# Samples' search bits start four gv tiles later and run in the chunks; turned rows, samples' attention and the first prompt scores are interleaved

## The chip, the cores and the metric

One core of one Trainium2 chip runs the whole program. The metric is the device time of one execution in microseconds (us), the median over the runs.

## What is computed

One layer of a hybrid decoder on 1024 prompt tokens and on 32 sample tokens (8 sequences of 4). Cut to what matters here:

```python
h = modulate(rms_norm(x, norm1_g), sh_a, sc_a)
gq, gk, gv, glog, gr, dq, dk, dv, iq, ik, iw = project_heads(h, w_in, ...)   # one projection
gla_state, go = gla_scan(...)                     # gated linear attention, here in chunks of 128 tokens
sc = indexer_scores(iq, iw, ik)                   # relu(iq.ik) weighted by iw, masked by causality
_, idx = top_k(sc, 256)                           # each query attends to its 256 best keys
attn = softmax(dq . dk[idx]) @ dv[idx]            # samples: keys and values from paged caches
mix = concat([gla_output(go, gr, gla_norm_g), attn])
x = x + g_a * (mix @ w_out)
x = x + g_m * hmoe(modulate(rms_norm(x, norm2_g), sh_m, sc_m))   # 16 experts, top 2 in a group
```

## The kernel before, in words

Everything is float32 and every engine has an order of its own, written out by hand; engines meet by semaphores only. An engine does its instructions in that order, so a wait in one of them holds all that stand behind it.

**Top 256 by search.** A cut is sought for each query, bit by bit, 15 high bits and 16 low bits. VectorE does it for the prompt's tiles (`seek_high`, `seek_low`, L2069 to L2090, counting at L1994). For the samples ScalarE does it in `samp_bit` (L1614): count signs (L1621), compare (L1622), move the cut (L1624). The first 15 of the 31 sample bits stand among the gate projections. The 16th, the first low bit, waits for `s_samp_key` at 2, which VectorE raises (L2069) when it has searched all high bits and built the keys of the low ones.

**The projections.** `project(n)` (L930 to L994) makes a tile in PSUM bank n % 2 and waits until `keep(n - 2)` on ScalarE has copied the tile made in the same bank; gv is kept at L1543. The gv jobs are tile 0, a part for the samples, tiles 1 to 7 and the samples' own tile. In `keep`'s loop (L1666) a sample bit follows each of the last seven jobs (`n >= first_gr - 7`).

**The chunks (L1098 to L1188 on TensorE, L1680 to L1704 on ScalarE, L2155 to L2200 on VectorE).** For each of 8 chunks of 128 tokens, and for the samples as a ninth: scores of linear attention (L1110), turned keys (L1118, copied at L1683), the projection gr (L969, kept through a silu at L1547), in chunks 4 to 7 also a dq tile (L992), outputs (L1145, L1146), the state's update (L1166). VectorE masks the scores (L2162), does two steps of its low search, updates the state and scales the chunk before (`mix_gla`, L2108). ScalarE squares the outputs (L1697), and does two sample bits in chunk 0 and one in each later chunk. VectorE's factors for chunk 0 are ready with the scaled gq and gk (L2095, L2097).

**After the chunks.** VectorE finds the cuts and makes masks (`make_mask`). TensorE turns the samples' cached keys (`turn_k`, L1204), scores the first four sequences (`score_set(0)`, L1211), then the last four (`score_set(1)`), adds the masks and the samples' own keys (L1241 to L1244), turns the nine tiles of linear attention (`turn_mix_g`, L1232, copied by `keep_mix_g`, L1724, in banks 2 and 3) and then turns the samples' probabilities (L1251, L1252). VectorE gives the minimum of each half (L2207), ScalarE the exponents (L1732, L1734), the copies of the turned probabilities (L1742, L1743), the scaled output (L1747) and its 16 small copies into `mix_t` (L1754), after which it raises `s_o_samp_kept`.

**Prompt attention.** 64 units of a query tile and a head. TensorE makes two at a time (`score_pair`, L1263), VectorE adds the mask and takes the minimum (`mask_and_min`, L2231), ScalarE exponentiates (L1764), VectorE scales by the sum (`normalise`, L2240), TensorE turns (`turn`, L1295) and weighs (`weigh`, L1305). The first `turn` needs four scaled units. Before, TensorE makes pair 0 ahead of the samples' products (L1278); pairs 2 to 6 and VectorE's first unit stand behind `s_o_samp_kept`.

After that come the output projection (L1352), the router and 24 steps of experts (L1416 to L1452).

Of the kernel before, what the change touches and what calls it, by code (L numbers as in the profile page):

```python
# [16 lines left out]
P = 128  # L17
D = 1024
KT = D // P
SEQ = 1024  # L20
NSEQ = 8
DT = 4
NS = NSEQ * DT
NT = SEQ // P
TILES = NT + 1
TOK = SEQ + NS
PAGES = 8
PAST = PAGES * P
LS = PAST + NS
# [6 lines left out]
HD = 64  # L36
GQ = 4
# [109 lines left out]
def hybrid_decoder_step(nc, place, a, a_out):  # L147

    jobs, first_gla, first_gr, first_dq = projections()
# [9 lines left out]
    with ExitStack() as ctx:  # L159
# [103 lines left out]
        psum = ctx.enter_context(nc.psum_tensor("psum", [P, 8, 512], F32))  # L263
# [626 lines left out]
        def _(pe):  # L890
# [316 lines left out]
            def score_set(half):  # L1207
                pe.wait_ge(s_k_seq_t, SET * (half + 1))
                for c in range(2):
                    for b in range(SET * half, SET * (half + 1)):  # L1210
                        mm = pe.matmul(psum[rows_of_seq(b), 4 + 2 * half + c, :], dq_samp[:, b, :], k_seq_t[:, b % SET, c * 512:(c + 1) * 512],  # L1211
                                       start=True, stop=False)
                mm.then_inc(s_k_seq_used, 1)
# [6 lines left out]
            score_set(0)  # L1220
            for b in range(SET + 1, NSEQ):
                turn_k(b)
            score_set(1)

            def turn_mix_g(i):

                r = rows(i)
                pe.wait_ge(s_mix_g, i + 1)
                if i >= 2:
                    pe.wait_ge(s_mix_g_t, i - 1)  # L1230
                for k in range(4):
                    t = pe.transpose(psum[:, 2 + i % 2, k * r:(k + 1) * r], gv[0:r, i, k * P:(k + 1) * P], ident[0:r, 0:r])  # L1232
                t.then_inc(s_mix_g_turned, 1)


            pe.wait_ge(s_k_seq_t, NSEQ)
            pe.wait_ge(s_masks, NT - 1)
            for half in range(2):
# [3 lines left out]
                pe.matmul(psum[:, half, 0:NS], dq_samp[:, SET * half:SET * (half + 1), :].rearrange("p b r -> p (b r)"), dk_t[:, SEQ:TOK],  # L1242
                          start=True, stop=False)
                pe.matmul(psum[:, half, 0:NS], visible, score[NT][0:NS, PAST:LS], start=False, stop=True).then_inc(s_samp_scores, 1)  # L1244
            for i in range(TILES):
                turn_mix_g(i)
            pe.wait_ge(s_mix_g_t, TILES)
            for half in range(2):
                pe.wait_ge(s_p_samp_exp, half + 1)
                for p in range(PAGES):  # L1250
                    t = pe.transpose(psum[:, 4 + 2 * half + p // 4, (p % 4) * P:(p % 4 + 1) * P], p_samp[:, half, p * P:(p + 1) * P], ident)  # L1251
                t = pe.transpose(psum[0:NS, 2 + half, 0:P], p_samp[:, half, PAST:LS], ident)  # L1252
                t.then_inc(s_p_samp_turned, 1)
            def score_pair(u):

                i, g, _, _ = unit_of(u)
# [10 lines left out]


            pe.wait_ge(s_p_samp_t, 2)
            score_pair(0)  # L1270
            for half in range(2):
                o = psum[:, 4 + 2 * half, 0:P]
                pe.matmul(o, p_samp_t[0:NS, half, PAGES, :], dkv[0:NS, NT, P:2 * P], start=True, stop=False)
                for b in range(SET * half, SET * (half + 1)):
                    wait_pages(b, 2)
                for p in range(PAGES):
                    for b in range(SET * half, SET * (half + 1)):
                        mm = pe.matmul(o[rows_of_seq(b), :], p_samp_t[:, half, p, rows_of_seq(b)], pages_of(b)[:, p, :],  # L1278
                                       start=False, stop=(p == PAGES - 1))
                mm.then_inc(s_o_samp, 1)  # L1280
            for half in range(2):
                pe.wait_ge(s_o_samp_rows, half + 1)
                pe.transpose(psum[:, 5 + 2 * half, 0:P], o_samp[:, half, :], ident).then_inc(s_v_pages_used, 1)
# [14 lines left out]
            def weigh(m):  # L1298
# [7 lines left out]
                                   start=(b == 0), stop=(b == groups[k][0][slot]))  # L1306
                mm.then_inc(s_weighed, 1)

            pe.wait_ge(s_o_samp_kept, 1)
            for u in range(2, PER_GROUP, 2):  # L1310
                score_pair(u)
            OUT_PART_AT = len(turns) - 5

            def out_products():
# [161 lines left out]
        def _(act):  # L1476
# [188 lines left out]
            keep_ada(2, ada_m1)  # L1665
            for n in range(first_gv + 1, first_gr):  # L1666
                keep(n)
                if n >= first_gr - 7:
                    samp_bit(*next(samp_next))

            squared = []
# [6 lines left out]
            for c in range(TILES):  # L1678
                r = rows(c)
                act.wait_ge(s_gla_k_turned, c + 1)  # L1680
                if c >= 2:
                    act.wait_ge(s_kv, c - 1)
                act.activation(k_rows[0:r, c % 2, :, :], psum[0:r, 4, 0:2 * P].rearrange("p (j k) -> p j k", j=2), copy).then_inc(s_gla_k_kept, 1)  # L1683
                keep(job_of["gr", c, 0])
                if ("dq", c - GQ, 0) in job_of and c - GQ >= 0:
                    keep(job_of["dq", c - GQ, 0])
                if c == NT - 1:
                    keep(job_of["gr_part", 0, 0])
                if c == NT:
                    act.wait_ge(s_inter, 1)  # L1690
                    act.activation(inter_rows.rearrange("p s v -> p (s v)"), psum[:, 3, :], copy).then_inc(s_inter_kept, 1)
                act.wait_ge(s_o, c + 1)
                act.wait_ge(s_kv, c + 1)
                if c >= 1:
                    own.wait(squared[-1])
                for h in range(H_GLA):
                    n = own.did(act.activation(squares[0:r, h * DV:(h + 1) * DV], psum[0:r, 5 + c % 2, h * DV:(h + 1) * DV], ACT.Square, accum_out=ss_g[0:r, c, h:h + 1]))  # L1697
                squared.append(n)
                act.activation(gv[0:r, c, :], psum[0:r, 5 + c % 2, :], copy).then_inc(s_o_kept, 1)
                if c >= 1:  # L1700
                    rstd_gla(c - 1)
                if c < NT:
                    for _ in range(2 if c == 0 else 1):
                        samp_bit(*next(samp_next))  # L1704
            rstd_gla(TILES - 1)
            assert next(samp_next, None) is None
# [18 lines left out]
                               scale=gla_g[:, 0:1]).then_inc(s_mix_g_t, 1)  # L1725

            act.wait_ge(s_w_small, 128)
            for half in range(2):
                for i in range(3 * half, 3 * half + 3):
                    keep_mix_g(i)  # L1730
                act.wait_ge(s_samp_min, half + 1)
                act.activation(p_samp[:, half, 0:PAST].rearrange("p (c s) -> p c s", c=2), psum[:, 4 + 2 * half:6 + 2 * half, :], ACT.Exp,  # L1732
                               scale=-1.0, bias=p_min[:, half:half + 1], accum_out=p_sum[:, 2 * half:2 * half + 1])
                act.activation(p_samp[:, half, PAST:LS], psum[:, half, 0:NS], ACT.Exp,  # L1734
                               scale=-1.0, bias=p_min[:, half:half + 1], accum_out=p_sum[:, 2 * half + 1:2 * half + 2]).then_inc(s_p_samp_exp, 1)
            for i in range(6, TILES):
                keep_mix_g(i)
            act.wait_ge(s_states_out, 64)
            act.wait_ge(s_mix_g, TILES)
            for half in range(2):  # L1740
                act.wait_ge(s_p_samp_turned, half + 1)
                act.activation(p_samp_t[:, half, 0:PAGES, :].rearrange("p (c k) r -> p c (k r)", c=2), psum[:, 4 + 2 * half:6 + 2 * half, :], copy)  # L1742
                act.activation(p_samp_t[0:NS, half, PAGES, :], psum[0:NS, 2 + half, 0:P], copy).then_inc(s_p_samp_t, 1)  # L1743
            act.wait_ge(s_p_inv, 1)
            for half in range(2):
                act.wait_ge(s_o_samp, half + 1)
                act.activation(o_samp[:, half, :], psum[:, 4 + 2 * half, 0:P], copy, scale=p_sum[:, 2 * half:2 * half + 1]).then_inc(s_o_samp_rows, 1)  # L1747
            for half in range(2):
                act.wait_ge(s_v_pages_used, half + 1)
                for n in range(2):  # L1750
                    of_head = psum[n * HD:(n + 1) * HD, 5 + 2 * half, 0:P].rearrange("p (b n g t) -> p n g b t", b=SET, n=2, g=GQ)[:, n]
                    at_tokens = slice(SEQ + half * SET * DT, SEQ + (half + 1) * SET * DT)
                    for g in range(GQ):
                        kept = act.activation(mix_t[n * HD:(n + 1) * HD, 4 + g, at_tokens].rearrange("p (b t) -> p b t", t=DT), of_head[:, g], copy)  # L1754
            kept.then_inc(s_o_samp_kept, 1)

            def exponent(u):

# [21 lines left out]
            o_after = {GROUP_BLOCKS * k + (pair[0] if slot == 0 else GROUP_BLOCKS - 1) + KEPT_AFTER: (k, slot)  # L1782
                       for k, (pair, n) in enumerate(groups) for slot in range(2)}

            for u in range(PER_GROUP):
                exponent(u)
            for m, (k, slot, b) in enumerate(turns):
                step = m % GROUP_BLOCKS
# [83 lines left out]
        def _(dve):  # L1872
# [40 lines left out]
            n = 0  # L1913
# [325 lines left out]
                own.wait(own.did(dve.reciprocal(a_inv[:, u:u + 1], a_sum[:, i, head:head + 1])))  # L2239
                dve.tensor_scalar(x, x, a_inv[:, u:u + 1], None, ALU.mult).then_inc(s_prob, 1)  # L2240

            dve.wait_ge(s_o_samp_kept, 1)
            mask_and_min(0)
            mask_and_min(1)
            for u in range(len(units)):
                if u + 2 < len(units):
                    mask_and_min(u + 2)
                normalise(u)
# [209 lines left out]
```

## Time and profile before

| | us |
|---|---|
| median of 3 runs | 1238.65 (1238.35 to 3723.86) |
| profiled execution, whole | 1239.81 |
| its span, first to last instruction | 1238.1 |
| TensorE busy | 1073.4 |
| VectorE busy | 617.0 |
| ScalarE busy | 401.3 |

The mean granted clock of TensorE is 0.926 of full speed. In the rows PE is TensorE's matmuls (transposes too), DVE is VectorE, ACT is ScalarE. A float32 product of full size shows as two records. "idle before" in brackets is the time in which the engine did nothing ahead of an instruction, with the one that ended it. Times in a timeline are us from the start of the span.

### The profile page before, as it was taken

The numbers are of one execution on the slowest core, as the hardware profiler recorded it, in microseconds if no ns is written. First come the engines' busy times: TensorE is split into PE (matmuls) and PEld (weight loads), VectorE is DVE, ScalarE is ACT, GpSimd is POOL, SyncE is SP. The second block draws the span as 40 slices with busy tenths as digits, with TensorE's granted clock in tenths as the row PEclk, the third lists the DMA queues.
The fourth block names the chain that finished last, engine by engine and source line by source line (L and its number), as shares of the span: only waits on it lengthen the run. The fifth ranks groups of instructions, "written<-read, shape, count | busy, mean of one in ns | idle before, by whom it ended". The sixth has DMA issues, their size and how long they took to land. (4 is left out here: it accounts for less than half of the span.)

```text
span 1238.1 us, 15189 instructions
## 1 busy us (share of the span) xinstructions
PE 1073.4 (87%) x4998; PEld 519.6 (42%) x4998; DVE 617.0 (50%) x1311; ACT 401.3 (32%) x880; POOL 121.8 (10%) x197
## 2 busy tenths in 40 slices
PE   4799999994998998986999999994699999999910
PEld 2595433341454544453444445553333333333300
DVE  3300589999299887933666423326112222222239
ACT  5321563640544343154777611112111111111113
POOL 0302000000000000522000000000211111111041
PEclk9799999997998997987999999996699999999965
DMA  9512516520310003346200111113897774576556
GB/s 342 192 39 57 204 35 238 206 71 0 72 30 0 1 1 85 90 137 163 58 1 1 35 38 70 62 56 124 315 366 279 301 293 182 209 268 255 187 213 241
DMA packets 70486, 170.82 MB, mean 138 GB/s; under 512 B 25511, under 2 KB 39959, under 8 KB 60041
## 3 DMA queue, kind: packets, MB, share of 16 engines
q1 hardware_dynamic: 55916, 122.77, 28.3%
q0 software_dynamic: 14496, 47.12, 10.6%
q8 instruction: 40, 0.66, 0.2%
q14 instruction: 34, 0.28, 0.1%
HBM read 237.18 MB, written 23.91 MB: 211 GB/s over the span
## 5 line engine op out<-in xcount | busy, mean ns | idle before, releaser
L969 PE MATMUL psum<-mem 128*128 128x512 f32 (+4 forms) x544 | 165.0, 462 | 24.9 <-ACT mem L1543 18.9
L1428 PE MATMUL psum<-mem 128*64 128x512 f32 x768 | 173.6, 606 | 3.7 <-DMA mem<-in_w_exp_up 2.5
L992 PE MATMUL psum<-mem 128*128 128x512 f32 x320 | 140.6, 596 | 0.0
L969 PEld LDWEIGHTS psum<-mem 128*128 128x128 f32 (+1 forms) x544 | 92.7, 192 | 90.6 <-issue 64.7
L1352 PE MATMUL psum<-mem 128*128 128x512 f32 x256 | 111.1, 593 | 0.6 <-issue 0.6
L1428 PEld LDWEIGHTS psum<-mem 128*64 128x64 f32 x768 | 54.1, 139 | 105.4 <-issue 101.3
L992 PEld LDWEIGHTS psum<-mem 128*128 128x128 f32 x320 | 60.1, 190 | 78.8 <-issue 78.0
L1452 PE MATMUL psum<-mem 128*64 128x512 f32 x384 | 87.6, 598 | 2.4 <-DVE mem L2396 2.4
L2404 DVE TENSOR_TENSOR mem<-psum,mem 128x256 f32<-128x256 f32 x24 | 10.2, 425 | 150.4 <-ACT mem L1849 150.4
L1994 DVE TENSOR_SCALAR_CACHE_REDUCE marks<-mem,top_try_low 128x384 uint16<-128x384 uint16 (+2 forms) x96 | 84.5, 942 | 0.6
L1994 DVE TENSOR_SCALAR_CACHE_REDUCE marks<-mem,top_try 128x384 bf16<-128x384 bf16 (+2 forms) x90 | 79.2, 942 | 0.5
L2394 DVE SCALAR_TENSOR_TENSOR mem<-psum,mem 128x1024 f32<-128x1024 f32 x24 | 30.8, 1284 | 90.9 <-PE psum L1452 90.9
L2231 DVE CUSTOM_DVE_ANT_0 mem<-psum,mem 128x1024 f32<-128x1024 f32 (+7 forms) x64 | 48.2, 754 | 55.3 <-PE psum L1263 40.0
L1352 PEld LDWEIGHTS psum<-mem 128*128 128x128 f32 x256 | 48.2, 190 | 58.8 <-issue 58.8
L1849 ACT ACTIVATE mem<-psum 128x256 f32<-128x256 f32 x24 | 9.2, 385 | 164.8 <-PE psum L1428 164.8
L1772 ACT ACTIVATE mem<-psum 128x512 f32<-128x512 f32 x72 | 42.8, 595 | 36.0 <-PE psum L1295 35.4
L1263 PE MATMUL psum<-mem 64*128 64x512 f32 (+3 forms) x192 | 42.6, 553 | 12.8 <-DVE a_min L2231 11.3
L1764 ACT ACTIVATE mem<-mem,a_min 128x1024 f32<-128x1024 f32 (+7 forms) x64 | 49.4, 771 | 6.4 <-DVE a_min L2231 6.3
L1295 PE MATMUL psum<-const,mem 128*128 128x128 f32 x288 | 48.0, 290 | 1.9 <-DVE mem L2240 1.9
L1922 DVE TENSOR_SCALAR mem<-mem,iw 128x512 f32<-128x512 f32 (+3 forms) x10 | 4.4, 437 | 87.8 <-ACT mem L1575 87.8
L1305 PE MATMUL psum<-mem 128*64 128x256 f32 x288 | 47.0, 405 | 0.1
L1805 ACT ACTIVATE mem<-mem 128x1024 f32<-128x1024 f32 (+1 forms) x9 | 9.5, 1056 | 111.4 <-DVE mem L2271 111.4
(385 smaller groups left out, 1420.6 us busy)
## 6 DMA issues: line engine op xcount, KB each, us to landing
mem<-in_w_exp_gate SPq DMA_DIRECT2D x48, 1024.0 KB
mem<-in_w_exp_up SPq DMA_DIRECT2D x48, 1024.0 KB
mem<-in_w_exp_down SPq DMA_DIRECT2D x48, 1024.0 KB
mem<-in_w_ada SPq DMA_DIRECT2D x24, 1024.0 KB, 10.0
y_of_slot<-mem POOLq DMA_DIRECT2D x24, 512.0 KB, 4.2
mem<-in_x_prompt SPq DMA_DIRECT2D x16, 512.0 KB, 5.0
mem<-in_w_in SPq DMA_DIRECT2D x3, 2048.0 KB, 7.7
h_rows<-mem POOLq DMA_DIRECT2D x8, 512.0 KB, 2.9
```

What stands on the lines that cost most here:

```text
L969: mm = pe.matmul(bank[0:rows(i), to:to + width], h_t[:, k, cols(i)], w[:, k, c0:c0 + width], start=(k == 0), stop=(k == KT - 1))
L992: mm = pe.matmul(bank[:, 0:n_t], w[:, k, c0:c0 + P], h_t[:, k, t0:t0 + n_t], start=(k == 0), stop=(k == KT - 1))
L1263: mm = pe.matmul(psum[:, score_bank(u + n) + s0 // 512, 0:w], dq_t[kv(n), g, cols(i)], dk_t[kv(n), s0:s0 + w], start=True, stop=True)
L1295: t = pe.transpose(psum[:, 4 + m % 2, q * P:(q + 1) * P], x[:, b * P:(b + 1) * P], ident)
L1305: mm = pe.matmul(psum[kv(n), 6 + slot, 0:2 * P], dkv[:, b, P + n * HD:P + (n + 1) * HD], prob_t[:, m % 3, 2 * n * P:2 * (n + 1) * P], star ...
L1352: mm = pe.matmul(psum[0:r, 2 * (i % 2) + c, :], mix_t[:, k, cols(i)], w_out[:, k, c * 512:(c + 1) * 512], start=(k == 0), stop=(k == KT - 1))
L1428: mm = pe.matmul(psum[half_rows(half), 2 + u, :].rearrange("p (n f) -> p n f", n=2), x_slot_t[:, u, k, half_rows(half)], gate_up_w[2 * u + ...
L1452: mm = pe.matmul(psum[half_rows(half), 6 + c, :], hid_t[:, u, m, half_rows(half)], down_w[2 * u + half][:, m, c * 512:(c + 1) * 512], star ...
L1764: act.activation(x, x, ACT.Exp, scale=-1.0, bias=a_min[:, i, head:head + 1], accum_out=a_sum[:, i, head:head + 1]).then_inc(s_exp, 1)
L1772: act.activation(prob_t[:, m % 3, :], psum[:, 4 + m % 2, :], copy).then_inc(s_turn_kept, 1)
L1994: dve.tensor_scalar(marks[0:r, j % 2, 0:width].bitcast(values[j].dtype), values[j], cuts[0:r, j:j + 1], None, ALU.is_ge, ALU.add, accum_ou ...
L2231: dve.tensor_tensor_reduce(x, banks, score[i], 1.0, 3 * BIG, ALU.add, ALU.min, a_min[:, i, head:head + 1]).then_inc(s_row_min, 1)
```

## The change

Four of the samples' search bits leave the gv tiles: there, bits now follow only the last three jobs, and chunks 1 to 4 have two bits instead of one. TensorE turns two tiles of linear attention ahead of `score_set(1)`, two after each half of the sample scores, and the last three around the turned probabilities, whose last piece now goes to bank 0 or 1. `score_pair(2)` follows the samples' products of half 0; TensorE waits for `s_o_samp_kept` only after `score_pair(6)`, VectorE only ahead of unit 8. ScalarE's exponents, copies of turned rows and of the samples' output follow the new order. No DMA issue is moved.

```diff
# TensorE
-            score_set(1)
...
+            def turn_p_samp(half):
+                pe.wait_ge(s_p_samp_exp, half + 1)
+                for p in range(PAGES):
+                    pe.transpose(psum[:, 4 + 2 * half + p // 4, (p % 4) * P:(p % 4 + 1) * P], p_samp[:, half, p * P:(p + 1) * P], ident)
+                pe.transpose(psum[0:NS, half, 0:P], p_samp[:, half, PAST:LS], ident).then_inc(s_p_samp_turned, 1)
+
+            pe.wait_ge(s_k_seq_t, NSEQ - 1)
+            turn_mix_g(0)
+            turn_mix_g(1)
+            score_set(1)
             pe.wait_ge(s_k_seq_t, NSEQ)
             pe.wait_ge(s_masks, NT - 1)
             for half in range(2):
...
-            for i in range(TILES):
-                turn_mix_g(i)
-            pe.wait_ge(s_mix_g_t, TILES)
-            for half in range(2):
-                pe.wait_ge(s_p_samp_exp, half + 1)
...
+                turn_mix_g(2 + 2 * half)
+                turn_mix_g(3 + 2 * half)
+            turn_p_samp(0)
+            turn_mix_g(6)
+            turn_p_samp(1)
+            turn_mix_g(7)
+            turn_mix_g(8)
...
             pe.wait_ge(s_p_samp_t, 2)
+            pe.wait_ge(s_mix_g_t, TILES)
             score_pair(0)
             for half in range(2):
...
                 mm.then_inc(s_o_samp, 1)
+                if half == 0:
+                    score_pair(2)
...
+            for u in range(4, PER_GROUP, 2):
+                score_pair(u)
             pe.wait_ge(s_o_samp_kept, 1)
-            for u in range(2, PER_GROUP, 2):
-                score_pair(u)
# ScalarE
             for n in range(first_gv + 1, first_gr):
                 keep(n)
-                if n >= first_gr - 7:
+                if n >= first_gr - 3:
                     samp_bit(*next(samp_next))
...
                 if c < NT:
-                    for _ in range(2 if c == 0 else 1):
+                    for _ in range(2 if c < 5 else 1):
                         samp_bit(*next(samp_next))
...
+            for i in range(4):
                 keep_mix_g(i)
             act.wait_ge(s_states_out, 64)
+            exponent_samp(0)
+            keep_mix_g(4)
+            keep_mix_g(5)
+            exponent_samp(1)
             act.wait_ge(s_mix_g, TILES)
+            keep_p_samp(0)
+            keep_mix_g(6)
+            keep_p_samp(1)
+            keep_mix_g(7)
+            keep_mix_g(8)
...
+            exponent(0)
+            exponent(1)
             act.wait_ge(s_p_inv, 1)
+            keep_o_samp(0)
+            exponent(2)
+            keep_o_samp(1)
+            exponent(3)
             for half in range(2):
                 act.wait_ge(s_v_pages_used, half + 1)
...
             kept.then_inc(s_o_samp_kept, 1)
-            for u in range(PER_GROUP):
+            for u in range(4, PER_GROUP):
                 exponent(u)
# VectorE
-            dve.wait_ge(s_o_samp_kept, 1)
             mask_and_min(0)
             mask_and_min(1)
             for u in range(len(units)):
+                if u + 2 == PER_GROUP:
+                    dve.wait_ge(s_o_samp_kept, 1)
                 if u + 2 < len(units):
                     mask_and_min(u + 2)
                 normalise(u)
```

`exponent_samp`, `keep_p_samp` and `keep_o_samp` hold the same instructions that stood in ScalarE's loops over the halves; before, its order was three copies of turned rows, exponents of half 0, three copies, exponents of half 1, three copies, then the turned probabilities, the outputs and all exponents of the first eight units.

## Rows read from the trace of the kernel before

**Rows 1.** The page, busy time: us, share of the span, instructions.
```profile
PE 1073.4 (87%) x4998; PEld 519.6 (42%) x4998; DVE 617.0 (50%) x1311; ACT 401.3 (32%) x880; POOL 121.8 (10%) x197
```

**Rows 2.** Waits, 260 to 600 us: engine, line, waited for, us, times, longest.
```profile
ACT mem L1621 <- DVEq L2069: 29.4, 1, 29.4
...
PE psum L969 <- ACT mem L1543: 18.9, 1, 18.9
...
DVE mem L2231 <- ACT mem L1754: 15.3, 1, 15.3
```

**Rows 3.** Timeline of TensorE, gv tiles: start, us, instruction, idle before.
```profile
264.03 27.73 PE L969 MATMUL psum<-mem 128*128 128x512 f32 x64
310.68 22.44 PE L969 MATMUL psum<-mem 128*128 128x512 f32 x48 [18.91 <-ACT mem L1543]
...
334.02 1.48 PE L1110 MATMUL psum<-mem 64*128 64x128 f32 x8
```

**Rows 4.** Timeline of ScalarE, the first low search bit.
```profile
308.08 1.17 ACT L1621 ACTIVATE mem<-mem,samp_shift 32x1056 bf16<-32x1056 uint16 x1 [29.41 <-DVEq L2069]
...
309.70 0.29 ACT L1624 ACTIVATE samp_shift<-samp_keep,samp_shift 32x1 f32<-32x1 f32 x1
```

**Rows 5.** Timeline of VectorE, the scaled gk.
```profile
310.55 2.35 DVE L2097 TENSOR_TENSOR mem<-mem 128x2112 f32<-128x2112 f32 x1
```

**Rows 6.** Timeline of ScalarE, chunks 2, 3 and 5: table, silu of gr.
```profile
366.37 1.28 ACT L1547 ACT_TABLE_LOAD   x1 [1.73 <-DVE mem L2108]
...
382.23 1.28 ACT L1547 ACT_TABLE_LOAD   x1 [5.10 <-DVE mem L2108]
...
420.00 0.60 ACT L1547 ACTIVATE mem<-psum 128x512 f32<-128x512 f32 x1 [1.82 <-PE psum L969]
```

**Rows 7.** Timeline of TensorE, chunk 3 and the gr tile of chunk 4.
```profile
383.19 0.46 PE L1145 MATMUL psum<-mem 128*128 128x128 f32 x2 [2.97 <-DVE mem L2162]
...
391.36 9.24 PE L969 MATMUL psum<-mem 128*128 128x512 f32 x16
```

**Rows 8.** Timeline of TensorE, from sample scores to the first turned probabilities.
```profile
536.54 1.93 PE L1211 MATMUL psum<-mem 128*32 128x512 f32 x16 [1.11 <-ACT mem L1718]
...
544.06 5.08 PE L1232 MATMUL psum<-const,mem 128*128 128x128 f32 x20
...
561.16 1.99 PE L1263 MATMUL psum<-mem 64*128 64x512 f32 x8 [1.26 <-ACT mem L1743]
...
572.32 2.86 PE L1263 MATMUL psum<-mem 64*128 64x512 f32 x8 [3.76 <-DVE a_min L2231]
...
581.56 1.12 PE L1295 MATMUL psum<-const,mem 128*128 128x128 f32 x4 [1.89 <-DVE mem L2240]
582.60 3.79 PE L1263 MATMUL psum<-mem 64*128 64x512 f32 x8
```

**Rows 9.** Timeline of ScalarE, turned rows and samples' attention.
```profile
545.27 1.48 ACT L1724 ACTIVATE mem<-psum,gla_g 128x512 f32<-128x512 f32 x2 [8.78 <-PE psum L1232]
...
549.23 1.11 ACT L1732 ACTIVATE mem<-psum,p_min 128x1024 f32<-128x1024 f32 x1
...
558.22 1.03 ACT L1742 ACTIVATE mem<-psum 128x1024 f32<-128x1024 f32 x1 [2.35 <-PE psum L1252]
...
568.07 1.58 ACT L1754 ACTIVATE mem<-psum 64x16 f32<-64x16 f32 x16
```

**Rows 10.** Timeline of VectorE, samples' minimum and first units.
```profile
541.09 1.23 DVE L2207 TENSOR_REDUCE p_min<-psum 128x1 f32<-128x1024 f32 x1 [7.63 <-PE psum L1244]
...
569.79 1.23 DVE L2231 CUSTOM_DVE_ANT_0 mem<-psum,mem 128x1024 f32<-128x1024 f32 x1 [15.26 <-ACT mem L1754]
...
576.49 0.75 DVE L2240 TENSOR_SCALAR mem<-mem 128x1024 f32<-128x1024 f32 x1
```

**Rows 11.** Busy time by stretch (TensorE's alone; all engines): last PEclk, DMA, GB/s.
```profile
544.00:549.00 5.00, 4.91 (x21) 0.50 0.46 130
...
411.30:471.00 59.70, 59.36 (x212) 30.34 (x212) 45.92 (x127) 24.03 (x58) 0.00 (x0) 1.00 0.00 0
```

More of the change, by code:

```diff
@@ L1244, in _ @@
                 pe.matmul(psum[:, half, 0:NS], visible, score[NT][0:NS, PAST:LS], start=False, stop=True).then_inc(s_samp_scores, 1)
-            for i in range(TILES):
-                turn_mix_g(i)
-            pe.wait_ge(s_mix_g_t, TILES)
-            for half in range(2):
-                pe.wait_ge(s_p_samp_exp, half + 1)
[L1250 to L1253, printed above, removed]
+                turn_mix_g(2 + 2 * half)
[5 more added lines that the diff above has]
+            turn_mix_g(8)
             def score_pair(u):
@@ L1727, in _, with exponent_samp @@
             act.wait_ge(s_w_small, 128)
-            for half in range(2):
-                for i in range(3 * half, 3 * half + 3):
-                    keep_mix_g(i)
+            def exponent_samp(half):
                 act.wait_ge(s_samp_min, half + 1)
@@ L1735, in _, with keep_p_samp @@
                                scale=-1.0, bias=p_min[:, half:half + 1], accum_out=p_sum[:, 2 * half + 1:2 * half + 2]).then_inc(s_p_samp_exp, 1)
-            for i in range(6, TILES):
+            def keep_p_samp(half):
+                act.wait_ge(s_p_samp_turned, half + 1)
+                act.activation(p_samp_t[:, half, 0:PAGES, :].rearrange("p (c k) r -> p c (k r)", c=2), psum[:, 4 + 2 * half:6 + 2 * half, :], copy)
+                act.activation(p_samp_t[0:NS, half, PAGES, :], psum[0:NS, half, 0:P], copy).then_inc(s_p_samp_t, 1)
@@ L1737, in _, with keep_o_samp @@
+            def keep_o_samp(half):
+                act.wait_ge(s_o_samp, half + 1)
+                act.activation(o_samp[:, half, :], psum[:, 4 + 2 * half, 0:P], copy, scale=p_sum[:, 2 * half:2 * half + 1]).then_inc(s_o_samp_rows, 1)
+            for i in range(4):
                 keep_mix_g(i)
             act.wait_ge(s_states_out, 64)
+            exponent_samp(0)
+            keep_mix_g(4)
+            keep_mix_g(5)
+            exponent_samp(1)
             act.wait_ge(s_mix_g, TILES)
[L1740 to L1754, printed above, removed]
@@ L1755, in _ @@
-            kept.then_inc(s_o_samp_kept, 1)
+            keep_p_samp(0)
[3 more added lines that the diff above has]
+            keep_mix_g(8)
             def exponent(u):
@@ L1783, in _ @@
                        for k, (pair, n) in enumerate(groups) for slot in range(2)}
-            for u in range(PER_GROUP):
+            exponent(0)
+            exponent(1)
+            act.wait_ge(s_p_inv, 1)
+            keep_o_samp(0)
+            exponent(2)
+            keep_o_samp(1)
+            exponent(3)
+            for half in range(2):
+                act.wait_ge(s_v_pages_used, half + 1)
+                for n in range(2):
+                    of_head = psum[n * HD:(n + 1) * HD, 5 + 2 * half, 0:P].rearrange("p (b n g t) -> p n g b t", b=SET, n=2, g=GQ)[:, n]
+                    at_tokens = slice(SEQ + half * SET * DT, SEQ + (half + 1) * SET * DT)
+                    for g in range(GQ):
+                        kept = act.activation(mix_t[n * HD:(n + 1) * HD, 4 + g, at_tokens].rearrange("p (b t) -> p b t", t=DT), of_head[:, g], copy)
+            kept.then_inc(s_o_samp_kept, 1)
+            for u in range(4, PER_GROUP):
                 exponent(u)
```

## The prediction

> **What bounds the kernel now.** I read four views, in this order. The page first: TensorE is busy for 87% of the span, so what can be won is TensorE's waits and its half-clock stretches; work taken off another engine is worth only what TensorE waited for it [rows 1]. Then the sums of waits between 260 and 600 us, the stretch that the diff touches. The reader is to see a ring there: ScalarE stood 29.4 us for VectorE's search keys, and TensorE 18.9 us for ScalarE, once each; and later VectorE stood 15.3 us for ScalarE's copies of the samples' attention [rows 2]. Then the timelines of the three engines, to see who was late at each place. Last, granted clock by stretch.
>
> The sum is made on the profiled execution: 1239.8 us, of which 1238.1 is its span; the median of the runs, 1238.65, is 1.2 below it.
>
> **Part 1: the search bits (gv tiles and chunks).** TensorE had finished gv tiles 1 to 4 at 291.8, 6.93 us a tile, and could not start tile 5 before ScalarE kept tile 3. ScalarE stood ahead of that copy in the first low search bit, waiting for the keys, until 308.08. So TensorE ran on at 310.68: 22.44 us for tiles 5 to 7, then 0.9 for the samples' tile, and chunk 0 at 334.02 [rows 3, 4]. The change starts the low bits behind tile 6 instead of tile 2. Then all copies that TensorE needs are made in time. Tiles 5 to 7 follow at 291.8 and take 3 x 6.93 = 20.8, to 312.6; with 0.9 for the last, chunk 0 is reached at 313.5, against 334.02: 20.5 us earlier. (18.9 is the wait; the rest is that the three tiles after it took 22.44 instead of 20.8, at a lower clock.)
>
> Two things could hold the new start. Chunk 0 needs VectorE's scaled keys gk, whose instruction begins at 310.55 and takes 2.35, so it ends at 312.9 [rows 5]: 0.6 us before TensorE comes, nothing late. And ScalarE meets its keys at 308.08, as now, but its first bit (1.95 us: 308.08 to 309.99 in [rows 4]) then ends at 310.0, before tile 7 is done at 312.6. VectorE's search itself is not touched: it idled between 312.9 and chunk 0, and that idle goes.
>
> What is added: one more bit of 1.95 us on ScalarE in each of chunks 1 to 4, ahead of the next chunk's copy of keys and its silu. What hides them is the wait that ScalarE has ahead of its silu: 1.73 us behind chunk 1's bit, 5.10 behind chunk 2's, 1.82 behind chunk 4's [rows 6]; behind chunk 3's it is like chunk 2's. So at most 0.2 shows on ScalarE, and TensorE, which then has a tile of nearly 7 us ahead of it, doesn't see it. Cost 0; if the cover failed everywhere, 4 x 1.95 = 7.8. TensorE's 2.97 us wait for VectorE in chunk 3 [rows 7] stays, because both engines start chunk 0 in the same relation as before (VectorE free first, TensorE's first product 1.5 us later). I bound it from +3 (gone) to -3 (twice). No DMA is moved by the diff; the dq weights and the sample states, loaded at the end of gv, have the same chunks of time before their use as now.
>
> **Part 2: turned rows and samples' attention.** Times are on the axis of before; part 1 shifts them all. Before, TensorE starts sample scores 1 at 536.54 after 1.11 us of waiting, turned rows run from 544.06, and prompt pair 0 starts at 561.16 [rows 8]. ScalarE's own work sets how early pair 0 can come, so I lay it out in the new order. The two rows turned ahead of scores 1 (8 transposes; 20 took 5.08 at half clock, so some 0.13 each at full) fill the 1.1 us wait and move nothing. VectorE's minimum of half 0 starts at 541.1 and is there 1.5 later, at 542.6 [rows 10]; it had stood idle 7.6 us, so the masks are no limit. ScalarE has copied four turned rows by 542.9 (0.74 each), loads its table, 1.28 (duration as in [rows 6]), and exponentiates half 0 in 1.36 (1.11 and the small second piece): 545.5. Two copies: 547.0. Half 1: 548.4. Turned half 0, 1.2 (1.03 and its small piece): 549.6. Row 6: 550.3. Turned half 1: 551.5. Rows 7 and 8: 552.7 [rows 9]. TensorE turns half 0 between 545.6 and 547.8 even at half clock, and half 1 by 550.7: hardly late. Pair 0 at 552.9 instead of 561.16: 8.2 us.
>
> **Part 3: the first prompt units.** VectorE's first masked row started only at 569.79, after 15.3 us of idle, because it waited for the last of the 16 small copies of the samples' output, which began at 568.07 and took 1.58 [rows 9, 10]. That wait moves to unit 8. Now it waits for pair 0's scores alone: 552.9 + 1.6 = 554.5, that is 15.3 earlier. From the first masked row to the first turned probabilities (581.56) it took 11.8. In the new order TensorE does samples' products of half 0 meanwhile, until 557.3, and so pair 2 begins 0.3 after its banks are free; the pair takes 1.99 like pair 0 instead of 2.86 [rows 8]. So 11.8 + 0.3 - 0.9 = 11.2, and turning starts at 565.7: 15.9 earlier in parts 2 and 3 together (8.2 and 7.7). What is late next is VectorE's chain of four masked units of 1.2 and four scalings of about 0.9 (0.75 and a reciprocal, [rows 10]); ScalarE's extra work between exponents ends, with the 16 copies, at about 565.2, so TensorE's wait for it, now ahead of the first turn, is hidden by 0.5. If that cover is gone, each us of it is paid.
>
> **The clock.** Between 544 and 549 the clock was 0.50 though TensorE was busy 4.91 of 5 us [rows 11], and pair 8 behind the first turn took 3.79 us where pair 0 of the same shape took 1.99: the lower of the two levels, 1.2 instead of 2.4 GHz, after waits of 3.76 and 1.89 us and another between them [rows 8]. The new order leaves waits of about 2 us there. I take 1 of the 1.8 us; at full clock throughout it is 1.8, at half clock from 553 on it is a loss of some 9 (2 for each of two pairs, 2.3 for each half's products).
> The Trainium skill (TensorE: Matmul & The Clock Gate, "What's actually happening") says that the throttled state is the default and that activity releases it. Taken alone it would give the whole 1.8, and the sum would be 1201.6. The row at 544 does not agree, since there the clock was low on a busy engine. That is why I don't count on it.
>
> **Sum.** 20.5 + 15.9 + 1 = 37.4. 1239.8 - 37.4 = 1202.4; I say 1202.
>
> **The rivals.**
> A. ScalarE's added bits do lie on the path of the chunks (7.8 us back): 1210. For it: in chunk 4 the cover is 1.82 against 1.95. Against: in the others VectorE is later. 12%.
> B. Half clock through the samples' stage (9 + 1 back): 1212. For it: [rows 11]. 13%.
> C. More than counted: chunk 3's wait goes too, and with it the slow stretch behind it, in which one gr tile took 9.24 us instead of 6.93 and the small products were slow too [rows 7] (3 + 4): 1195. 8%.
> D. Part 3 is hidden anyway: TensorE's wait for the samples' copies moves with it and holds the first turn as before, and parts 2 and 3 give nothing: 1239.8 - 20.5 = 1219. Against: 0.5 us of cover and a queue in which the exponents stand ahead of the copies. 4%.
> E. It does not do what it says: ScalarE's wait for the keys, now behind tile 6, is met by TensorE again because VectorE comes later, say at 314 or more, and most of part 1 stays away: about 1220. Against: nothing that VectorE does before 312.9 is moved. 2%.
> F. The other side: the chunks with dq fall to half clock. In 59.7 us there TensorE is busy 59.36, at 1.00 [rows 11]; at half they last 59.7 longer: 1202 + 60 = 1262, slower than before. It decides as soon as over 37.4 us of such work runs at half. For it: the slow tile of [rows 7]. Against: it was one tile, and this stage has the same work as before. 2%.
>
> My forecast has the other 59%. The range takes in A, B and C: 1195 to 1213. A measurement of this kernel can tell about 2% (24.8 us) from no change; faster than 1214 holds in my forecast and A to C, 92%; D and E lie within 2%, 6%; F is slower, 2%.
>
> **What would show it.** Right: no TensorE wait over 1 us among the gv tiles; chunk 0 at about 313.5; ScalarE's wait for the keys about 2 us; from the start of chunk 0 to the start of the dq jobs behind the chunks the same length as before; VectorE's first masked row 15 us earlier in relation to the turned keys, and pair 8 near 2 us. Wrong: waits of TensorE for ScalarE in chunks 1 to 4 (A), 0.50 in the clock between sample scores and first turn (B), a wait of many us ahead of the first turn (D). If parts 1 to 3 show as worked out and the time is still not near 1202, something behind 590 moved, which I hold for a plain shift.

## The result, and the profile after

The changed kernel takes 1203.76 us (median) beside 1239.12 for the kernel before; the ratio is 0.9708, 95% interval 0.9684 to 0.9732. Each of the two medians is over four executions, one of which (2967 and 3724 us) was far slower and is not in the ratio; the other three alone have medians of 1202.62 and 1238.65. The profiled execution took 1202.62, with a span of 1200.9. A second set of runs, e5 below, gave 1202.47 beside 1240.96, ratio 0.9686 (0.9670 to 0.9702). Forecast were 1202 and a range of 1195 to 1213.

The page of the changed kernel: the span, TensorE's row, which answers to [rows 1], and the granted clock in 40 slices.

```profile
span 1200.9 us, 15186 instructions
...
PE 1066.6 (89%) x4998; PEld 516.6 (43%) x4998; DVE 617.0 (51%) x1311; ACT 401.1 (33%) x880; POOL 122.4 (10%) x197
...
PEclk9799999999997997999999999995799999999965
```

The number of instructions on TensorE, VectorE and ScalarE is the same, and so, within 0.2 us, is what VectorE and ScalarE are busy for. TensorE is busy 6.8 us less with the same work, because more of it ran at the full clock. The other 30 us are time in which TensorE no longer waits.

TensorE's timeline of the changed kernel, in the places of [rows 3, 7 and 8] (start, us, instruction, idle before it):

```profile
263.14 48.33 PE L969 MATMUL psum<-mem 128*128 128x512 f32 x112
...
312.38 1.47 PE L1110 MATMUL psum<-mem 64*128 64x128 f32 x8
...
349.85 1.48 PE L1110 MATMUL psum<-mem 64*128 64x128 f32 x8
...
361.54 0.49 PE L1145 MATMUL psum<-mem 128*128 128x128 f32 x2 [2.97 <-DVE mem L2185]
...
368.20 2.49 PE L1110 MATMUL psum<-mem 64*128 64x128 f32 x8
...
371.10 9.21 PE L969 MATMUL psum<-mem 128*128 128x512 f32 x16
...
504.35 1.95 PE L1204 MATMUL psum<-const,mem 128*128 128x128 f32 x16
...
525.58 1.92 PE L1237 MATMUL psum<-const,mem 128*128 128x128 f32 x8
...
532.04 1.99 PE L1269 MATMUL psum<-mem 64*128 64x512 f32 x8 [1.37 <-ACT mem L1733]
...
545.01 0.63 PE L1304 MATMUL psum<-const,mem 128*128 128x128 f32 x4 [2.42 <-DVE mem L2263]
545.88 3.56 PE L1269 MATMUL psum<-mem 64*128 64x512 f32 x8 [0.25 <-DVE a_min L2254]
```

The gv tiles 1 to 7 are one block of 48.33 us (6.90 a tile) with no wait in it, where [rows 3] shows two blocks and 18.91 between them. Three more rows of the kernel before are needed to lay the two beside each other, the starts of chunks 3 and 4 and of the turned keys:

```profile
371.50 1.48 PE L1110 MATMUL psum<-mem 64*128 64x128 f32 x8
...
388.45 2.49 PE L1110 MATMUL psum<-mem 64*128 64x128 f32 x8
...
524.64 1.95 PE L1204 MATMUL psum<-const,mem 128*128 128x128 f32 x16
```

| stretch of the profiled execution | before | after | difference | forecast |
|---|---|---|---|---|
| start to chunk 0 | 334.0 | 312.4 | -21.6 | -20.5 |
| chunk 0 to the turned keys | 190.6 | 192.0 | +1.4 | 0 |
| turned keys to pair 0 | 36.5 | 27.7 | -8.8 | -8.2 |
| pair 0 to the first turn | 20.4 | 13.0 | -7.4 | -7.7 |
| first turn to the end of the span | 656.5 | 655.9 | -0.6 | -1 |
| span | 1238.1 | 1200.9 | -37.2 | -37.4 |

Of the 21.6, 0.9 stood already ahead of gv tile 1 (264.03 and 263.14) and has nothing to do with the change; 20.7 are part 1. The last stretch took 655.9 to 658.2 us in the traces of this document, 657.4 in the second execution of the changed kernel (e5), so its 0.6 is inside what executions differ by.

ScalarE of the changed kernel, in the places of [rows 4 and 9]:

```profile
307.18 1.17 ACT L1630 ACTIVATE mem<-mem,samp_shift 32x1056 bf16<-32x1056 uint16 x1 [1.94 <-DVEq L2092]
...
522.76 1.28 ACT L1739 ACT_TABLE_LOAD   x1
524.05 1.12 ACT L1739 ACTIVATE mem<-psum,p_min 128x1024 f32<-128x1024 f32 x1
...
525.42 1.26 ACT L1733 ACTIVATE mem<-psum,gla_g 128x512 f32<-128x512 f32 x2
...
543.00 1.58 ACT L1806 ACTIVATE mem<-psum 64x16 f32<-64x16 f32 x16
```

Its wait for the keys is 1.94 us instead of 29.41. The copies at 525.42 follow the exponents with no table load between, so mixing the two kinds of work costs no load: there is one, 1.28 us, as before. The Trainium skill (ScalarE: Activation LUTs, "Table sets: the hidden batching unit") says why that can be: cheap functions such as copy are in every set, and only a change of set costs a load. The rows here agree with it.

VectorE of the changed kernel, in the places of [rows 10]; the last row is the scaling that the first turn waits for:

```profile
520.88 1.23 DVE L2230 TENSOR_REDUCE p_min<-psum 128x1 f32<-128x1024 f32 x1 [7.72 <-PE psum L1252]
...
534.13 1.23 DVE L2254 CUSTOM_DVE_ANT_0 mem<-psum,mem 128x1024 f32<-128x1024 f32 x1 [5.69 <-PE psum L1269]
...
544.08 0.79 DVE L2263 TENSOR_SCALAR mem<-mem 128x1024 f32<-128x1024 f32 x1
```

Its 15.26 us wait for the samples' copies is now 5.69 us for pair 0's scores.

### The profile page after: what moved, and what is told of

The parts are those of the page before. It is cut to its first block and busy times, and to the rows that moved or that the text cites. A ratio compares the mean times of both kernels' runs of the same rounds, so it can differ in the third digit from the quotient of the medians.

```text
span 1200.9 us, 15186 instructions
## 1 busy us (share of the span) xinstructions
PE 1066.6 (89%) x4998; PEld 516.6 (43%) x4998; DVE 617.0 (51%) x1311; ACT 401.1 (33%) x880; POOL 122.4 (10%) x197
```

## The experiments

**Each half alone.** e1 is the kernel before with the search bits moved, e2 the changed kernel with them back:

```diff
# e1, on the kernel before
-                if n >= first_gr - 7:
+                if n >= first_gr - 3:
-                    for _ in range(2 if c == 0 else 1):
+                    for _ in range(2 if c < 5 else 1):
# e2, on the changed kernel: the same two lines the other way
```

> The kernel before with the search bits moved alone (part 1), the order of turned rows and first units as before. My theory: chunk 0 is reached some 20.5 us earlier, nothing is paid for the four bits in chunks 1 to 4 beyond up to 1.5 us of a longer half-clock stretch in chunk 3: 1239 - 20 = 1219, between 1217 and 1221. Rival A (the four bits lie on the path of the chunks): 1226. Rival E (the wait for the keys is only put elsewhere): above 1230.

> The changed kernel with the search bits at their old places (parts 2 and 3 alone). My theory: 8.5 us from sample scores to pair 0, 7.5 from pair 0 to the first turn, 0 to 1 behind it: 1239 - 16 = 1223, between 1221 and 1225, and the gains of this run and of the bits alone add up to the whole within 2 us. Rival D (part 3 hidden): 1231.

Measured: e1 1218.84 (0.9825, 0.9806 to 0.9844), e2 1221.82 (0.9857, 0.9835 to 0.9880), beside 1239.70. That is 20.9 and 17.9 us; their sum, 38.8, is the 38.5 of the second set of runs within 0.3, and 2.8 more than the 36.0 of the first (1238.65 less 1202.62). So the two halves add up as closely as the two sets agree. Rivals A (1226), E (above 1230) and D (1231) fall. In e1 VectorE's first masked row still waits for the samples' copies, even 17 us, the old wait with its full length:

```profile
549.25 1.22 DVE L2231 CUSTOM_DVE_ANT_0 mem<-psum,mem 128x1024 f32<-128x1024 f32 x1 [17.14 <-ACT mem L1754]
```

**Where the bits may start.** e3 and e4 start them behind gv tiles 4 and 5 instead of tile 6:

```diff
# e3: 5 and c < 3; e4: 4 and c < 4
-                if n >= first_gr - 3:
+                if n >= first_gr - 5:
-                    for _ in range(2 if c < 5 else 1):
+                    for _ in range(2 if c < 3 else 1):
```

> The changed kernel with the first low bit behind gv tile 4 instead of tile 6 (five bits among the gv tiles, two in chunks 0 to 2 only). My theory: ScalarE stands from tile 4's copy to the keys at 307.2, takes 1.95 for the bit, and copies tile 5 at about 309.1 to 309.7; TensorE wants its bank at 304.5 for tile 7. So TensorE waits 5.2 us and the time is 5 to 7 us above the changed kernel: 1208 to 1210. If the place of the bits among the gv tiles does not matter as I worked it out (the gain came from something else), it equals the changed kernel, 1203.

> The same with the first low bit behind gv tile 5 (four bits among the gv tiles, two in chunks 0 to 3). ScalarE then copies tile 6 at 309.7, and TensorE wants that bank only for the samples' tile at 311.4. My theory: no wait, the time equals the changed kernel within 1 us: 1203. A rival by which every tile that the bits come earlier costs its 7 us: 1206 to 1210.

Measured: e3 1210.80, just above the 1208 to 1210 that I expected, and e4 1205.18. The waits, between 255 and 600 us, of e3 and then of e4 (us in total, times, longest):

```profile
ACT mem L1630 <- DVEq L2092: 15.7, 1, 15.7
...
PE psum L969 <- ACT mem L1552: 5.2, 1, 5.2
```

```profile
ACT mem L1630 <- DVEq L2092: 8.8, 1, 8.8
```

ScalarE waits 15.7 us in e3 and TensorE 5.2 of them; in e4 ScalarE still waits 8.8 and TensorE none. That is the place from which the ring costs: two banks let TensorE be two tiles ahead, and a wait of ScalarE shorter than that lead is free. What I had left out is the clock behind the wait. The gv tile that follows it in e3 takes 8.68 us instead of 6.90, so the wait of 5.2 costs 7.0 in all:

```profile
311.80 8.68 PE L969 MATMUL psum<-mem 128*128 128x512 f32 x16 [5.17 <-ACT mem L1552]
```

e4's median is 2.6 and 2.7 above the two of the changed kernel (1202.62 and 1202.47), inside the spread of its own runs (1199.6 to 1207.1).

**What cover the four bits have.** e6 does each sign count of chunks 1 to 4 twice, which changes no result; e5 is the changed kernel itself beside it.

```diff
                         samp_bit(*next(samp_next))
+                        if 1 <= c < 5:
+                            own.wait(own.did(act.activation(samp_marks, samp_keys[1], ACT.Sign, ..., accum_out=samp_signs[:, 0:1])))
```

> The changed kernel itself, run beside the other three of this set so that they can be compared on one chip: 1203 to 1204.

> The changed kernel with the sign count of every search bit in chunks 1 to 4 done twice on ScalarE (same result), 8 more counts of about 1.25 us in all, 2.5 us a chunk. It prices the cover that part 1 leans on. My theory: ScalarE's copies of keys come 2.5 us later but before TensorE's state products, and its silu ends before the squares' turn in chunks 1 to 3; TensorE sees nothing or up to 2 us in all: 1203 to 1206. Rival A (ScalarE's bits lie on the path): 8 x 1.25 = 10, 1213.

Measured: e5 1202.47, e6 1202.42. Ten more us on ScalarE cost nothing; rival A is gone. ScalarE in e6, from the silu in chunk 2 to the squares of the same chunk's outputs:

```profile
350.66 0.60 ACT L1556 ACTIVATE mem<-psum 128x512 f32<-128x512 f32 x1
351.82 0.28 ACT L1706 ACTIVATE mem<-psum 128x128 f32<-128x128 f32 x1 [0.57 <-issue]
```

It reaches the squares with 0.57 us to spare, where the changed kernel has 3.17 us. They begin at the same distance from the start of the chunk, 12.66 us. So the cover beyond the four bits is some 3 us in this chunk; what TensorE would pay once it is gone was not tried.

**The wait in chunk 3.** Before and after, TensorE waits 2.97 us in chunk 3 and is slow afterwards. e7 moves one of VectorE's search steps from chunk 3 to chunk 5, e8 besides moves ScalarE's bit of chunk 7 to chunk 5.

```diff
+            LOW_STEPS_AT = [0, 2, 4, 6, 7, 9, 12, 14, 16]      # e7, e8; in e9 [0, 2, 4, 5, 7, 9, 12, 14, 16]
-                    seek_low(c * LOW_BITS // NT, (c + 1) * LOW_BITS // NT)
+                    seek_low(*LOW_STEPS_AT[c:c + 2])
# e8 besides, on ScalarE
-                    for _ in range(2 if c < 5 else 1):
+                    for _ in range(2 if c < 6 else 7 - c):
```

> The changed kernel with VectorE's sixteen low search steps spread 2,2,2,1,2,3,2,2 over the chunks instead of 2 in each: one step of 6.4 us moved from chunk 3, where TensorE waits 3.0 us for VectorE and then runs at half clock, to chunk 5, where TensorE's dq tile gives VectorE 3 us of slack. Theory 1 (the wait sets off the half clock): the 3.0 us go and with them most of the slow stretch (the chunk took 18.4 us instead of 12.5, the next one 22.8 instead of 19.4): 1203.8 - 7 to 9 = 1195 to 1197. Theory 2 (the half clock has nothing to do with the wait): only 3 us: 1201. Theory 3 (the moved step is late in chunk 5 or at the samples' chunk): 1203 or more.

> e7 and, besides, no search bit on ScalarE in chunk 7 (two bits in chunks 0 to 5, one in chunk 6), so that ScalarE comes 1.95 us earlier to the samples' chunk, where TensorE waits 3.1 us for VectorE and then 2.1 for ScalarE. My theory: about 2 us less than e7: 1193 to 1195. Rival (VectorE's k_own and cuts set that place): equal to e7.

Measured: e7 1201.11, e8 1203.76; neither differs from e5 beyond the spread, and both expectations (1195 to 1197, 1193 to 1195) were missed. In e8 TensorE's wait for ScalarE in the samples' chunk did fall from 2.12 to 0.94 us, but the chunk became only 0.8 shorter, too little to show in the median. In e7 it was my edit that missed: the wait in chunk 3 is still there, unchanged.

```profile
362.54 0.46 PE L1145 MATMUL psum<-mem 128*128 128x128 f32 x2 [2.97 <-DVE mem L2186]
```

The mask for which TensorE waits stands ahead of chunk 3's own steps on VectorE, so only steps of chunks 0 to 2 can be late for it. e9 moves the step from chunk 2 to chunk 5.

> The changed kernel with VectorE's low search steps spread 2,2,1,2,2,3,2,2. e7 took a step out of chunk 3, but the mask that TensorE waits for there stands ahead of that chunk's steps, so the lag of VectorE was built in chunks 0 to 2 and the 2.97 us stayed. Here the step leaves chunk 2, and VectorE comes to chunk 3's mask 6.4 us earlier. Theory 1 (that wait sets off the half clock of the next 12 us): the wait goes and chunk 3 and 4 take 12.5 and 19.4 us instead of 18.4 and 22.8: 9 us less than the changed kernel, 1194. Theory 2 (the half clock comes anyway): 3 us less, 1200. Theory 3 (the lag comes back in chunk 5): as the changed kernel.

Measured: e9 1193.43, ratio to the kernel before 0.9604 (0.9585 to 0.9622), 9.0 below e5. Theory 1 holds. TensorE by stretch (us, busy, count, granted clock, DMA share, GB/s), the changed kernel and then e9:

```profile
349.85:358.40 8.55, 8.49 (x28) 1.00 0.00 0
361.50:368.20 6.70, 6.61 (x24) 0.52 0.00 0
368.20:371.10 2.90, 2.84 (x12) 0.50 0.00 0
371.10:380.15 9.05, 9.05 (x17) 0.76 0.00 0
380.15:390.96 10.81, 10.75 (x41) 1.00 0.01 2
```

```profile
349.50:362.50 13.00, 12.83 (x54) 1.00 0.00 0
362.50:382.00 19.50, 19.39 (x70) 1.00 0.00 1
```

With the wait, TensorE is busy all the time from 361.5 on, and still at the lower level (1.2 GHz) until inside the gr tile at 371.10. Without it the clock stays at 1.00 through both chunks. From the start of chunk 3 to that of chunk 5 TensorE took 41.1 us in the changed kernel and 31.85 in e9, so a 3.0 us wait cost 9.3 us: 3.0 of waiting and 6.3 of half clock. The other traces bear it out: the two kernels without the wait (e9, e11) took 31.9 for these chunks, the eleven with it 39.7 to 41.1, which prices it at 7.9 to 9.3.

**The samples' chunk.** e10 puts the first dq job ahead of TensorE's wait for the samples' mask and takes the bit out of chunk 7; e11 is e9 and e10 together.

```diff
                 if c == NT - 1:
                     project(job_of["gr_part", 0, 0])
+                if c == NT:
+                    project(first_dq)
...
-            for n in range(first_dq, n_jobs):
+            for n in range(first_dq + 1, n_jobs):
                 project(n)
# and on ScalarE as in e8
```

> The changed kernel with two edits at the samples' chunk: no search bit in chunk 7, and the first dq job (the samples' part, 3.3 us behind the chunk) put ahead of TensorE's 3.1 us wait for VectorE's mask. My theory: the wait is filled, 2 to 3 us for it, and about 1 for the bit, as e8's shorter wait for ScalarE (0.9 instead of 2.1) showed: 1199 to 1200. Rival: the chain there is VectorE's and ScalarE's, the job only moves: 1202.

> e9 and e10 together. Under theory 1 the gains add up: 9 + 3 = 12 us below the changed kernel, 1191, and 3.9% below the kernel before. Under theory 2: 1197.

Measured: e10 1196.51 (0.9635, 0.9618 to 0.9653), e11 1190.65 (0.9589, 0.9576 to 0.9602). e10 gained 6.0 where I expected 3. TensorE in the samples' chunk, the changed kernel and then e10:

```profile
456.13 1.08 PE L1135 MATMUL psum<-mem 128*32 128x128 f32 x32 [3.06 <-DVE mem L2192]
459.33 3.59 PE L1155 MATMUL psum<-mem,const 128*32 128x256 f32 x8 [2.12 <-ACT mem L1700]
462.85 1.91 PE L1158 MATMUL psum<-mem 32*32 32x128 f32 x8
464.69 7.09 PE L1179 MATMUL psum<-mem 32*64 32x128 f32 x64
```

```profile
455.69 1.08 PE L1137 MATMUL psum<-mem 128*32 128x128 f32 x32 [1.34 <-DVE mem L2194]
458.02 1.89 PE L1157 MATMUL psum<-mem,const 128*32 128x256 f32 x8 [1.26 <-ACT mem L1702]
459.84 1.06 PE L1160 MATMUL psum<-mem 32*32 32x128 f32 x8
460.83 4.36 PE L1181 MATMUL psum<-mem 32*64 32x128 f32 x64
```

From the start of the samples' chunk to the first of the last three dq tiles it is 25.9 us instead of 32.6, so the trace has 6.7 us. The two waits give 2.6 of them, and the half clock behind them comes later and costs less: the same 64 small products took 4.36 instead of 7.09. But that need not all be the edit's doing. e1 and e6 leave this chunk as it was and keep its 3.06 us wait, and took 30.6, with the half clock in another place. In e6:

```profile
465.61 4.44 PE L1179 MATMUL psum<-mem 32*64 32x128 f32 x64
```

So some 2 of the 6.7 us may be the place of the half clock, which I can't tell from the edit. e11 is the fastest kernel here, 11.8 us below the changed one and 50.3 below the kernel before. The gains of e9 and e10 add up to 15.0 and not to 11.8; the difference is smaller than the spread within the runs of either (6.8 and 7.8 us).

## Why the prediction was right

**Part 1.** 20.5 us forecast, 20.7 in the trace and 20.9 in the median of e1. The reading held in each step: the wait went as a whole because all copies that TensorE needs are made before ScalarE stops for the keys, and e3 and e4 place the border where the arithmetic had it (5.2 us of waiting forecast and found for tile 4, none for tile 5). The four added bits cost nothing, and e6 shows it rather than argues it.

**The chunks.** Forecast was a plain shift; it was 1.4 us longer, and that sits in chunk 3, which took 18.35 us instead of 16.95. The wait is the same 2.97. In the kernel before, the products behind it ran at full clock for about 2 us, to 385.4, and only then slowly; in the changed kernel the second one was slow already (0.79 us at 361.96). So the step that was mis-sized is "stays": the wait did stay, while its aftermath had no fixed length. I had put that wait at 3 us in the bounds, and at 7 with its slow stretch in rival C; e9 shows that it is worth 9.

**Part 2.** 8.2 forecast, 8.8 found. On the axis of before (20.3 later than after, by the turned keys) pair 0 stood at 552.3, forecast 552.9. ScalarE's queue did set the place, as the 1.37 us that TensorE waits for its last copy says.

**Part 3.** 7.7 forecast, 7.4 found. The first turn stands at 565.3 on that axis, forecast 565.7, and waits for VectorE's scaling (ends at 544.87), not for the samples' copies, which end at 544.58. So the 0.5 us of cover that I had counted was about 0.3: right, with little to spare.

**The clock.** This term was mis-sized. Of the 1.8 us for pair 8 I took 1; it took 3.56 us instead of 3.79, so 0.2 was given, and the sign "pair 8 near 2 us" did not come. It still has a wait of 2.42 us ahead of the turn. I had also argued that a rule could not be relied on, since the clock was 0.50 on a busy engine at 544. Chunk 3 shows how a busy engine can have it: the low clock begins up to 2 us after a wait and lasts through busy work behind it. In [rows 8] a wait of 1.11 us ends at 536.54, and that it caused the low clock at 544 is argued only. The changed kernel speaks against it. No such wait is left there, the longest between 504 and 530 us is 0.36, and the clock still fell. That wait, and then TensorE by stretch (columns as for e9):

```profile
506.65 1.98 PE L1204 MATMUL psum<-const,mem 128*128 128x128 f32 x16 [0.36 <-ACT mem L1727]
...
504.00:523.60 19.60, 18.50 (x126) 1.00 0.62 172
523.60:526.00 2.40, 2.29 (x15) 0.93 0.49 134
526.00:529.00 3.00, 3.00 (x16) 0.50 0.44 126
```

So one wait and the stretch behind it account for chunk 3, and what lowers the clock among the turned rows stays open. The Trainium skill (TensorE: Matmul & The Clock Gate, "What's actually happening") has throttled as the default and activity as what releases it. e9's trace agrees for the chunks, with 1.00 throughout once TensorE never rested there; the rows from 526 to 529, at 0.50 with TensorE busy throughout, show that being busy at the moment is not enough.

Rivals A, D and E fell with e6 and e1 to e4, and F with chunks 5 and 6, which took 19.4 us each, as before. B came in a small part: the clock was 1.00 from the turned keys to 523.6 and from 530 to 545, and 0.50 for some 3 us between. C did not come by this change but was real: in e9 the wait goes and the slow stretch with it.

**How much was luck.** The mechanism of parts 1 to 3 held step by step. That the span fell within 0.2 us of the sum was luck in part: 0.9 us of opening, 0.2 more in part 1 and 0.6 more in part 2 made up for most of the 1.4 lost in the chunks, 0.3 less in part 3 and 0.4 less of clock.

## What to carry to other kernels

An in-order engine that waits for one thing holds all the copies that stand behind it; ask for each wait how far ahead the engine that it feeds can run (here two banks, so two tiles), and place the wait inside that lead. Then price a wait of TensorE not by its length alone but together with the half clock that follows it: here 3.0 us cost 7.9 to 9.3, and 5.2 us cost 7.0. And before moving work to cure a lag, find the instruction that is waited for and move only what stands ahead of it in its queue: e7 moved a step from behind it and gained nothing.

## What the runs showed of the hardware that I had not expected

- A single wait of 2.97 us in an otherwise busy stretch was followed by some 13 us in which the clock was 0.50 (361.9 to 375.4), with TensorE busy throughout. It cost twice its own length on top (e9 against the changed kernel, 9.3 us in the two chunks).
- The place of the slow stretch is not fixed by the order of the work. In the changed kernel the turning of the samples' half 0 took 1.92 us (at 525.58); in e3, with the same order from there on, it took 1.09 and pair 0 took 2.94 instead of 1.99. The samples' chunk took 32.6 us in the traces of both kernels, e2, e3, e5 and e7, and 30.6 in e1 and e6, with the same 3.06 us wait in it. What sets the place was not tried.
- The same kernel reached chunk 0 at 312.4 in one execution and at 315.2 in another (e5, whose span was 1205.2). In the traces of the kernels that start the bits behind tile 5 or 6 it lay between 311.4 and 315.2. So 3 to 4 us of what separates two executions can lie in the opening, ahead of everything that the change touches; what does it there was not tried.
